# Local attention inside a two-layer encoder: the first stream tile of ten items moved ahead of the turns of probabilities

## What is computed

```python
def windowed_gqa(q, k, v, sink):
    ...
    s = jnp.einsum('bnqhgd,bnkhd->bnhgqk', qb, kw, preferred_element_type=jnp.float32) * (1.0 / math.sqrt(HEAD_DIM))
    ...
    m = jnp.maximum(jnp.max(s, axis=-1, keepdims=True), sink_l)
    p = jnp.exp(s - m)
    denom = jnp.sum(p, axis=-1, keepdims=True) + jnp.exp(sink_l - m)
    o = jnp.einsum('bnhgqk,bnkhd->bnqhgd', (p / denom).astype(v.dtype), vw)

def mlstm_group(u_qk, u_v, u_o, u_gates, conv_w, conv_b, gate_bias, norm_g):
    qk = jax.nn.silu(centred_dwconv(u_qk, conv_w, conv_b))
    ...
    return (h * jax.nn.sigmoid(u_o.astype(jnp.float32))).astype(u_o.dtype)
```

## Time and profile before

| | us |
|---|---|
| median of 3 runs | 2225.08 |
| lowest and highest run | 2221.23, 2226.53 |
| the profiled execution, its own time | 2230.33 |
| its span, first to last instruction | 2228.5 |
| PE busy in the span | 2104.0 (94%) |
| DVE busy | 1331.5 (60%) |
| ACT busy | 991.3 (44%) |
| mean granted TensorE clock | 0.979 of full |

### The profile page before, as it was taken

The page is one execution under the profiler, slowest core; times in us unless marked ns, Lnnn a source line. Parts: engine busy times, 40 slices in busy tenths (PEclk is TensorE's granted clock), DMA queues, the critical chain, the costliest instruction groups (busy, mean ns, idle before and its releaser), DMA issues.

```text
span 2228.5 us, 31496 instructions
## 1 busy us (share of the span) xinstructions
PE 2104.0 (94%) x11392; PEld 1699.3 (76%) x11392; DVE 1331.5 (60%) x2057; ACT 991.3 (44%) x1616; POOL 226.0 (10%) x268
## 2 busy tenths in 40 slices
PE   7989989999999899999798999999999989999997
PEld 7779967888887577777577897778887767777773
DVE  4875487722454765656877647783235476666557
ACT  3554565232422455555245557533333235555552
POOL 0000023000000421001100001300000032100004
PEclk9999999999998999999999999999999999999998
DMA  4154112321102699999511112033120069999995
GB/s 153 57 198 147 39 76 96 105 85 57 57 29 98 252 368 371 386 382 349 189 53 38 39 45 89 20 133 114 57 76 20 32 230 389 375 379 371 377 372 202
DMA packets 78531, 384.85 MB, mean 173 GB/s; under 512 B 10472, under 2 KB 11864, under 8 KB 43608
## 3 DMA queue, kind: packets, MB, share of 16 engines
q1 hardware_dynamic: 55264, 327.31, 38.8%
q0 software_dynamic: 10096, 30.38, 3.9%
q10 hardware_dynamic: 13064, 25.75, 3.1%
HBM read 352.27 MB, written 46.07 MB: 179 GB/s over the span
## 4 chain that ended last, share of the span: by engine, by line
PE 71%; DVE 15%; ACT 8%; issue 3%; DMA 2%; POOL 1%; DVEq 0%; ACTq 0%; POOLq 0%; SPq 0%
PE bank L2197 29%; PE bank L2709 9%; PE bank L2683 8%; PE bank L2673 7%; PE bank L2410 5%; PE bank L2441 2%; ACT scratch L1055 2%; PE bank L2520 2%; DVE scratch L1595 2%; PE bank L2218 1%; DVE weight_slots_parts L1433 1%; PE bank L2649 1%; PE bank L2564 1%; PE bank L2580 1%; DVE small L1601 1%
## 5 line engine op out<-in xcount | busy, mean ns | idle before, releaser
L1903 DVE TENSOR_TENSOR weight_slots_parts<-weight_slots,mixer_region_parts 128x2048 fp32r<-128x2048 f32 x140 | 322.2, 2322 | 84.9 <-ACT mixer_region_parts L1257 84.8
L2197 PE MATMUL bank<-weight_slots_parts,x_transposed_parts 128*128 128x256 f32 (+1 forms) x1248 | 300.3, 335 | 8.6 <-DVE mixed L1555 5.7
L2197 PE MATMUL bank<-x_transposed_parts,weight_slots_parts 128*128 128x512 f32 (+1 forms) x1024 | 265.1, 346 | 8.3 <-DVE mixer_region L1547 5.1
L1257 ACT ACTIVATE mixer_region_parts<-weight_slots 128x2048 fp32r<-128x2048 f32 x140 | 261.1, 1910 | 23.5 <-ACT x_transposed L1332 18.1
L1433 DVE TENSOR_TENSOR weight_slots_parts<-weight_slots,weight_slots_parts 128x2048 fp32r<-128x2048 f32 x58 | 133.0, 2292 | 193.6 <-ACT weight_slots_parts L950 192.8
L2709 PE MATMUL bank<-weight_slots,x_transposed 128*128 128x512 f32 x560 | 247.4, 595 | 0.1
L2197 PEld LDWEIGHTS bank<-weight_slots_parts,x_transposed_parts 128*128 128x128 f32 x1248 | 211.6, 194 | 28.0 <-DVE mixed L1555 6.5
L2683 PE MATMUL bank<-mixer_region_parts,x_transposed_parts 128*128 128x256 f32 x1120 | 207.5, 283 | 1.0 <-DVE weight_slots_parts L1903 0.9
L2197 PEld LDWEIGHTS bank<-x_transposed_parts,weight_slots_parts 128*128 128x128 f32 x1024 | 181.6, 194 | 31.5 <-DVE mixer_region L1547 6.4
L2673 PE MATMUL bank<-mixer_region_parts,x_transposed_parts 128*128 128x512 f32 x560 | 191.8, 414 | 4.6 <-DVE x_transposed_parts L1908 4.6
L2709 PEld LDWEIGHTS bank<-weight_slots,x_transposed 128*128 128x128 f32 x560 | 104.0, 191 | 118.5 <-issue 103.0
(11 more groups left out here) (319 smaller groups left out, 3577.7 us busy)
## 6 DMA issues: line engine op xcount, KB each, us to landing
weight_slots<-in_w_gate SPq DMA_DIRECT2D x70, 1024.0 KB, 7.4
weight_slots<-in_w_up SPq DMA_DIRECT2D x70, 1024.0 KB, 7.1
weight_slots<-in_w_down SPq DMA_DIRECT2D x70, 1024.0 KB, 8.0
weight_slots<-in_w_in SPq DMA_DIRECT2D x20, 1024.0 KB, 5.1
slots_y<-x_transposed ACTq DMA_DIRECT2D x66, 256.0 KB
weight_slots<-in_wkv_mem SPq DMA_DIRECT2D x16, 1024.0 KB, 4.8
slots_y<-in_consts SPq DMA_DIRECT2D x6, 2304.0 KB, 16.8
weight_slots<-in_w_out SPq DMA_DIRECT2D x8, 1024.0 KB, 4.8
```

The lines of the kernel that those rows point to most:

```text
L1257: nc.scalar.activation(hi, raw, ACT.Copy).then_inc(moe.high_ready, 1)
L1903: v.tensor_tensor(lo, raw, hi.bitcast(F32), ALU.subtract).then_inc(moe.low_ready, 1)
L2197: ins = pe.matmul(ps, lhs[i](k), rhs[j](k), start=k == 0 and a == 0, stop=k == KD - 1 and a == 2)
```

## The change

In items 1 to 10 (`tile_goes_first`) the first stream tile moves ahead of the turns, on PE and in DVE's and ACT's programs; the others keep their order. Items 0, 11 and 12 are as before. No instruction is added or removed, and no transfer, bank or semaphore changes.

- PE: scores, **tile 1**, wait for `p_ready`, turns, **tile 2**, value product, further tiles. Before: scores, wait for `p_ready`, turns, tile 1, value product, tiles 2 and on.
- DVE: the reciprocals (L1583, L1584), **tile 1** with the finish of the tile before it, then eviction of the scores and `m_ready`, tile 2, eviction of the value product, further tiles. Before, tile 1 stood behind `m_ready`.
- ACT: the silu or sigmoid chain of `ended` (and a split that hangs on it) moves from behind the exponentials to ahead of the copies of the turned blocks.

```diff
+def tile_goes_first(i):
+
+    return 0 < i < 11
...
@@ scalar engine
                         for t in ended:
                             if t[0] == "v":
                                 drain_values(t)
+                            if tile_goes_first(i):
+                                stream_tile(t)
                         if i:
...
-                        for t in ended + w[:-1] if i < 12 else ():
+                        for t in (w[:-1] if tile_goes_first(i) else ended + w[:-1]) if i < 12 else ():
...
@@ vector engine
                             step(v.reciprocal(st[:, ro:ro + 4], st[:, ro:ro + 4]))
+                        if tile_goes_first(i):
+                            stream_tile(w[0])
...
                         if w and i:
-                            stream_tile(w[0])
+                            stream_tile(w[1 if tile_goes_first(i) else 0])
...
-                        for t in w[1:]:
+                        for t in w[2 if tile_goes_first(i) else 1:]:
                             stream_tile(t)
...
@@ tensor engine
+                        if tile_goes_first(i):
+                            stream_tile(w[0])
                         if i:
                             pe.wait_ge(p_ready, 12 * l + i)
                             turn_probs()
                         if w and i:
-                            stream_tile(w[0])
+                            stream_tile(w[1 if tile_goes_first(i) else 0])
...
-                        for t in w[1 if i else 2:]:
+                        for t in w[2 if i == 0 or tile_goes_first(i) else 1:]:
                             stream_tile(t)
```

## The result

| | before | changed |
|---|---|---|
| median, us | 2224.74 (4 runs) | 2256.50 (4 runs) |
| lowest and highest, us | 2221.23, 2226.53 | 2255.22, 2258.01 |
| profiled execution, its own time and its span | 2230.33, 2228.5 | 2255.22, 2253.6 |
| mean granted TensorE clock | 0.979 | 0.975 |

The changed kernel takes 1.0145 times as long (95% interval 1.0127 to 1.0163), 31.8 us more by the medians.

A forecast was written before the change was run, and what follows sets the result against it. PE was taken as the bound, if other engines return its banks in time. Waits of 23.8 us plus 6.8 of lower clock made 30.6 us on the profile, less 5.2 from profiled execution to median: 2255 us, range 2240 to 2268.

The forecast's parts named there:

- Items 7 and 8: The third tile waits 2.8 us for ACT's eviction of the first tile's bank, twice: 5.6 us per layer.
- Item 6: Two turns and the first v tile wait 2.5, 3.2 and 2.1 us on DVE and ACT: plus 5.4 per layer.
- Item 9: The split that made the third tile wait is done early: minus 1.6 us per layer.
- Item 11: PE has a tile less before its turns; the last tile's wait grows from 1.3 to 2.8: plus 1.5 us per layer.
- Items 1 to 5: Item 3's p_ready wait goes, its copies' wait grows, item 4 waits more, items 1 and 5 less: plus 1.0 us per layer.
- The sum of the waits: In the attention of both layers, the item terms add 11.9 us per layer, 23.8 us for both.
- The clock: Behind new PE waits, two low-clock stretches per layer, each 3.4 us long and costing 1.7: 6.8 us for both layers.
- items 7 and 8 alone: Rival: only the waits at these items appear, 11.2 us, giving 2236 us (2232 to 2242); chance 0.13.
- The clock did fall at nearly every new wait: Rival: the clock falls at every new wait, 23.8 + 17 = 40.8 us, giving 2266 us; chance 0.14.
- The stop at item 3: Rival: this PE stop is really gone and no new waits come, 16.6 us gained, giving 2208 us; chance 0.05.

The follow-up runs named there:

- first_v_early: Changed kernel, but in items 6, 7 and 8 ACT evicts the first v tile ahead of the turned blocks' copies; 1.0082 times the kernel before.
- square_later: Changed kernel with ACT's square moved behind the evictions of the v tiles in items 7 and 8; 1.0120 times the kernel before.
- fill_item_6: Changed kernel with 18 and 22 unread matmuls on PE ahead of item 6's second and third turned block; 1.0139 times the kernel before.
- only_1_to_5: Changed kernel with the first tile ahead of the turns in items 1 to 5 alone; 1.0071 times the kernel before.
- only_6: Changed kernel with the first tile ahead of the turns in item 6 alone; 1.0037 times the kernel before.
- only_7_8: Changed kernel with the first tile ahead of the turns in items 7 and 8 alone; 1.0112 times the kernel before.
- only_9_to_11: Changed kernel with the first tile ahead of the turns in items 9, 10 and 11 alone; 1.0019 times the kernel before.
- the four parts: Changed kernel with the new order only in items 7 and 8, 6, 1 to 5, or 9 to 11; 1.0112, 1.0037, 1.0071, 1.0019 times the kernel before.
- fill_waits: Changed kernel with 18 unread matmuls on PE behind the value product in each of items 7 and 8; 1.0115 times the kernel before.

## Why the prediction was right

Slower by over 0.3%, the form of it and its size (2255 said, 2256.5 measured) held, the size in part by luck, as the steps show. By its steps, idle time per layer, layer 0 and then layer 1 from PE in order of time:

- **Items 7 and 8**: 5.6 us said, 2.59 + 2.58 = 5.2 measured in either layer, all for L1008. The count was 8.3 − 5.5 = 2.8 for each. From the turns to the tile behind the eviction it is 8.2 us as said (208.45 to 216.68); PE's own pieces last 5.65 and not 5.5, since the product was taken at 1.70 and is busy for 1.90. first_v_early and square_later show the mechanism.
- **Item 6**: waits of 2.5, 3.2 and 2.1 said; 2.31, 2.51 and 0.64 in layer 0, 2.31, 2.98 and none in layer 1. The first two are right, with their releasers. The third is the step that failed: its 2.1 took PE at full clock, and PE was at 0.50 and filled the wait itself. fill_item_6, with the clock held, has 1.94. The increase is 3.0 and 2.8 in place of 5.4. The first wait stands where it was put, and the count from item 5's first tile was the right one: only_1_to_5 has it and only_6 doesn't, so it is not item 6's own new order that makes it.
- **Item 9**: −1.6 said, −1.6 measured in both layers.
- **Item 11**: 2.8 said, 2.78 and 2.79 measured, from 1.27 and 1.29; +1.5 as said.
- **Items 1 to 5**: +1.0 said; −0.1 and +0.7 measured. As said, the wait for `p_ready` at item 3 vanished and the one for the copies behind it grew, from 1.22 to 2.97, so that the stop only moved.
- **The sum of the waits**: 23.8 said for both layers, 17.1 measured. The shortfall of 6.7 is item 6 (5.0) and for the rest items 1 to 5 and 7 and 8.
- **The clock**: 6.8 said, 12.0 measured. Two new low stretches per layer were taken. The low stretches last 44.4 us in the changed kernel against 20.5 in the kernel before, 7 pieces of 3.4 us more. Item 6 has two new pieces and items 7 and 8 one each, in both layers; layer 1 has one more at item 11, and one fewer at item 0 and at item 3. The prediction took two per layer where items 6 to 8 have four.

So 29.1 us measured in the stretches stand against 30.6 said, with waits 6.7 too high and clock 5.2 too low. The two errors are one and the same in part: PE's slow pieces at item 6 lay inside waits that had been counted as idle. For the rest it is luck that they cancel. The result also owes something to what lies outside: 3.9 us less in the profiled execution, and profiled executions that stand differently to their medians (before 5.6 above, changed 1.3 below).

The Trainium skill ("TensorE: Matmul & The Clock Gate", section "A second HAM failure mode: psum-queue depth-cycling"), which says that short idles between groups that cycle through banks make the clock swing, was nearer to this kernel than the value taken: the clock is low at each new wait of items 6, 7 and 8 in both layers, though not behind that of item 11 in layer 0, nor, in only_7_8, behind the 2.58 us of item 8 in layer 1.

Of the rivals, items 7 and 8 alone carry 15.8 of 29.1 us, so the other terms do exist. The clock did fall at nearly every new wait, but the waits were smaller than that rival's. The stop at item 3 stayed.

**What stays open.** The timed differences are not those of the stretches: only_7_8 is 24 us above the kernel before by the medians and 15.8 in the stretches, only_9_to_11 4 above and 1.9 below. By the medians the four parts add up to 51.6 us, where the whole change costs 31.8. The part of the program that no edit touches differs by up to 9 us between profiled executions, and no run was made that tells whether the shift in time itself does it. The record has one hint. The kernel before is quicker where its mean granted clock is higher (of 17 executions timed beside only_7_8, 2218.3 and 2220.0 us at 0.983 and 0.985, 2234.5 us at 0.978), and the profiled execution that all stretches are compared with is one of its longer ones, 2230.3 us at 0.979. So the timed differences may hold low clock, outside the stretches or in them, that the comparison of profiles doesn't show. How much was not measured.

## What to carry to other kernels

Where engines meet through a few banks in strict order, moving a piece of work ahead of a hand-over is free of instructions and not of time: for each bank, add up what stands on the producing engine between the hand-over and the next need of that bank, and what stands on the evicting engine between the same hand-over and its eviction. Here 5.5 us against 8.3, from a few rows, gave a wait of 2.8 before anything ran, and 2.6 was measured. If the order is wanted, take the eviction out of the chain that hangs on the hand-over: at items 7 and 8 it fitted into idle time of ACT, and the stretches were 16.5 us shorter. And look for a wait behind the items that were reordered: with items 1 to 5 alone in the new order, item 6 lost 10.2 us. So add up the parts of such a change item by item; a total that fits can be two errors.

## What the runs showed of the hardware

- The same idle time did not always bring the same clock. The wait of 1.86 us at the start of the stretch was followed by 0.50 in layer 0 and by 1.00 in layer 1 of the changed kernel. Busy time of the changed kernel, 3.4 us behind that wait in either layer:

```profile
83.90:87.30 3.40, 3.40 (x10) 2.67 (x9) 3.07 (x8) 0.00 (x0) 0.00 (x0) 0.52 0.00 0
1174.70:1178.10 3.40, 3.40 (x16) 2.80 (x15) 3.10 (x8) 0.00 (x0) 0.00 (x0) 1.00 0.02 5
```

  In the same time PE has got through 16 matmuls at 1.00 and through 10 at 0.52. The wait of 2.58 us at item 8 of layer 1 was followed by 0.50 in the changed kernel and by 1.00 in only_7_8. What decides was not settled.
- A low stretch behind a wait made an item about 1.5 us longer where PE set the time (items 7 and 8: 19.7 us with it, 18.2 without). Where another engine did, it cost next to nothing: in the changed kernel the low stretch at item 0 of layer 0 is missing in layer 1, and there PE waits 1.25 us more for DVE's L1554 in item 1, so that the scores of item 2 start 25.4 and 25.2 us behind those of item 0.
- Matmuls that compute nothing, in a wait of 2.6 us, held the clock at 1.00 and made items 7 and 8 of both layers 5.7 us shorter (fill_waits), where PE set the time behind the wait. Where another engine's chain did, the same filler gave nothing (fill_item_6: item 6 of layer 0 at 24.63 against 24.62 us).
